# A two-layer transformer block kernel: gate projections of the convolution moved among the heads, its norm into the output projections, and an opening in column groups

## What is computed

```
mod = silu(c) @ w_ada[l] + b_ada[l]                 # shift, scale, gate; the same for the context
h   = rms_norm(x, norm_g[l]) * (1 + scale) + shift
(a_glu, a_gate, nq, nk, nv, n_gate, wq, wk, wv, w_gate, merge) = split(h @ w_in[l])
# convolution branch
a   = a_glu[:, :512] * sigmoid(a_glu[:, 512:])
a   = silu(layer_norm(depthwise_conv(a, 31 taps), cln_g, cln_b))
y_a = (a * silu(a_gate)) @ w_proj_a
# neighbourhood attention (the leading branch, 8 heads of 64) and window attention
y_b = (o_na * silu(n_gate)) @ w_proj_b
y_c = (o_wa * silu(w_gate)) @ w_proj_c
y   = sigmoid(g_a) * y_a + sigmoid(g_b) * y_b + sigmoid(g_c) * y_c
x   = x + gate * (y @ w_o)
```

## Time and profile before

| | |
|---|---|
| median of three runs | 3160.3 us (3156.06 to 3160.52) |
| the profiled execution | 3154.38 us |
| its span, first to last instruction | 3152.6 us |
| mean granted TensorE clock | 0.995 |
| TensorE busy | 3042.8 us |
| VectorE busy | 1829.4 us |
| ScalarE busy | 1295.9 us |
| GpSimd busy | 263.3 us |

### The profile page before, as it was taken

One profiled execution on the slowest core, in us unless ns is written; L12 is line 12 of the kernel. 1 busy time (PEld: TensorE's weight loads), 2 busy tenths in 40 slices (PEclk: granted clock), 3 DMA queues, 4 the chain that ended last, 5 costly groups with the idle time before them and its releaser, 6 DMA issues.

```text
span 3152.6 us, 37117 instructions
## 1 busy us (share of the span) xinstructions
PE 3042.8 (97%) x14862; PEld 2399.3 (76%) x14862; DVE 1829.4 (58%) x2911; ACT 1295.9 (41%) x2007; POOL 263.3 (8%) x206
## 2 busy tenths in 40 slices
PE   8999999999999998999999999999999999999998
PEld 5877877877788677667777777788887876788887
DVE  5877675255435767684444786666436662566632
ACT  3244523135532344534454474322225667422222
POOL 0011100001100001102110021000003210000000
PEclk9999999999999999999999999999999999999999
DMA  5222132320012322222112233333332310233232
GB/s 207 73 67 74 48 104 92 109 86 28 21 34 77 108 80 77 67 81 69 50 51 78 80 96 94 94 94 94 95 96 86 114 38 1 76 97 95 94 94 74
DMA packets 78732, 251.52 MB, mean 80 GB/s; under 512 B 9120, under 2 KB 11168, under 8 KB 78560
## 3 DMA queue, kind: packets, MB, share of 16 engines
q1 hardware_dynamic: 72672, 227.91, 23.1%
q0 software_dynamic: 5024, 18.09, 1.9%
q10 hardware_dynamic: 864, 3.15, 0.3%
HBM read 247.01 MB, written 2.10 MB: 79 GB/s over the span
## 4 chain that ended last, share of the span: by engine, by line
PE 46%; ACT 4%; DVE 2%; issue 1%; DMA 0%; POOL 0%; DVEq 0%; ACTq 0%
PE PS L1158 32%; PE PS L1796 4%; PE PS L2816 3%; PE PS L2917 1%; PE PS L1920 1%; PE PS L2894 1%; ACT WH L1107 1%; PE PS L2895 1%; PE PS L2876 1%; PE PS L2877 0%; PE PS L2838 0%; ACT L1982 0%; PE PS L2544 0%; ACT L1984 0%; DVE WL L1117 0%
## 5 line engine op out<-in xcount | busy, mean ns | idle before, releaser
L1117 DVE TENSOR_TENSOR WL<-RAW,WH 128x1024 fp32r<-128x1024 f32 (+3 forms) x374 | 424.0, 1135 | 528.4 <-ACT WH L1107 527.6
L1107 ACT ACTIVATE WH<-RAW 128x1024 fp32r<-128x1024 f32 (+3 forms) x397 | 384.6, 972 | 436.0 <-PE PS L1158 332.1
L1796 PE MATMUL PS<-Hh,WH 128*128 128x512 f32 x1376 | 524.4, 381 | 14.5 <-DVE WL L1117 8.0
L1796 PE MATMUL PS<-Hl,WH 128*128 128x512 f32 x1376 | 486.6, 354 | 0.0
L1796 PE MATMUL PS<-Hh,WL 128*128 128x512 f32 x1376 | 485.7, 353 | 0.0
L1796 PEld LDWEIGHTS PS<-Hh,WH 128*128 128x128 f32 x1376 | 259.5, 189 | 74.2 <-issue 22.7
L1158 PE MATMUL PS<-XH,WH 128*128 128x512 f32 x768 | 305.0, 397 | 0.0
L1158 PE MATMUL PS<-XH,WL 128*128 128x512 f32 x768 | 303.4, 395 | 0.0
L1158 PE MATMUL PS<-XL,WH 128*128 128x512 f32 x768 | 303.4, 395 | 0.0
L1796 PEld LDWEIGHTS PS<-Hl,WH 128*128 128x128 f32 x1376 | 259.9, 189 | 47.7 <-issue 10.1
L1796 PEld LDWEIGHTS PS<-Hh,WL 128*128 128x128 f32 x1376 | 260.1, 189 | 40.3
(11 more groups left out here) (404 smaller groups left out, 5747.4 us busy)
## 6 DMA issues: line engine op xcount, KB each, us to landing
RAW<-in_w_in SPq DMA_DIRECT2D x124, 512.0 KB, 3.6
RAW<-in_ffn_in SPq DMA_DIRECT2D x96, 512.0 KB, 3.6
RAW<-in_ffn_out SPq DMA_DIRECT2D x48, 512.0 KB, 3.6
RAW<-in_w_ada SPq DMA_DIRECT2D x32, 384.0 KB, 3.7
RAW<-in_nsa_in SPq DMA_DIRECT2D x21, 512.0 KB, 3.3
RAW<-in_lru_in SPq DMA_DIRECT2D x20, 512.0 KB, 3.6
MW<-in_w_ada SPq DMA_DIRECT2D x32, 256.0 KB, 9.6
BS<-in_bs POOLq DMA_DIRECT2D x16, 512.0 KB, 3.9
```

Of the source, the lines that this page charges most:

```text
L1107: act.activation(WH[half[j]][:, 0:n], RAW[j % NRAW][:, 0:n], ACT.Copy).then_inc(*did("act_whi", ("whi", j)))
L1117: dve.tensor_tensor(WL[half[j]][:, 0:n], RAW[j % NRAW][:, 0:n], WH[half[j]][:, 0:n].bitcast(F32), ALU.subtract).then_inc(*did("dve_wlo", ( ...
L1796: mm = pe.matmul(ps[:, c:c + w_], wt[:, 128 * k:128 * k + 128], x[:, a:a + w_], start=(k == 0 and q == 0), stop=(k == n - 1 and q == 2))
```

## The change

In the planner, for layer 1's leading branch: a chunk `cg` of the convolution's gates follows `ag` in phases 1 to 4 (its eviction `cgev` is a Silu after its eighth step, with a reload of the exponential table behind it). The pins of the heads move from step 22 to 27 and that of `out` from 18 to 22. Behind the phases the order is mg3, pj0, pj1, mg4, pj2, mg5, pj3, mg6, pj4, mg7, pj5 to pj7, cm0, pa0, cm1, pa1, and `normed` puts `ln0` behind the last unit of taps, `ln1` four steps later, `lnv`, `ln2`, `ln3` after 10, 14 and 20 steps, and `ln4` one, three and five steps behind pj7. Four fillers go (15 matmuls, 30 instructions): before pv(1,0,0,1,3), max(1,0,2,0,3), pv(1,0,3,0,3) and mg7. The gates' buffer SG of layer 1 moves, and `cgev` in layer 1 no longer waits for the splits.

In the opening: a piece is four matmuls of 128 columns into four column groups, the row copy is four activations, the roots are copied to SBUF by ScalarE (`act_root0`), the first two weight loads go ahead of pieces 16 and 20, their splits come earlier, and `pe_first` computes cb(0,0) and ca(0,0) together, k by k, with pieces 24 to 27 behind k = 2, 28 to 31 behind k = 3 and turn 3 behind k = 4. ScalarE's row copy 2 stands before its first k and row copy 3 before k = 5.

```diff
 KEEP = {
...
-    ('pv', 1, 0, 0, 1, 3): 4,
-    ('max', 1, 0, 2, 0, 3): 2,
-    ('pv', 1, 0, 3, 0, 3): 4,
...
-    ('mg', 1, 0, 7): 5,
...
+        def gates(ph):
+            return [("cg", ph - 1, 1024)] if L else []
...
+            if kind == "cg":
+                return {8: [("cgev", nm)]}
...
-            ready = (25 if L else 19) if br else 22
+            ready = (25 if L else 19) if br else 27 if L else 22
...
-                chunks = [("aq", ph, cq), ("ag", ph - 1, cg), ("av", ph, cv), ("ak", ph + 1, ck) if ph < 3 else ("mg", 0, cm)]
+                chunks = [("aq", ph, cq), ("ag", ph - 1, cg)] + gates(ph) + [("av", ph, cv), ("ak", ph + 1, ck) if ph < 3 else ("mg", 0, cm)]
...
-                chunks = [("ag", 3, cg), ("mg", 1, cm), ("mg", 2, cm)]
+                chunks = [("ag", 3, cg)] + gates(ph) + [("mg", 1, cm), ("mg", 2, cm)]
...
-                    at.setdefault(1 if f else 22 if L and br else 18, []).extend(to)
+                    at.setdefault(1 if f else 22 if L else 18, []).extend(to)
...
+        def normed(units):
+            steps = {0: [("ln0", L)], 4: [("ln1", L)], 10: [("lnv", L)], 14: [("ln2", L)], 20: [("ln3", L)]}
+            begin = max(i for i, u in enumerate(units) if u[0] == "taps")
+            end = sum(u[0] == "lin" for u in units[begin:])
+            steps.update({end + 1: [("ln4", L, 0), ("ln4", L, 1)], end + 3: [("ln4", L, 2)], end + 5: [("ln4", L, 3)]})
+            for m in range(2):
+                units = units + conv_mixed(m)[0:8] + [("mgev", ("cm", L, 0, m))] + conv_mixed(m)[8:] + [("paev", ("pa", L, 0, m))]
...
-            tail += beside(proj(m)) + (beside(merge(m + 4)) if m < 4 else [])
+            ahead_ = m + 3 if L and 1 <= m < 5 else m + 4 if m < 4 and not L else None
+            tail += beside(proj(m)) + (beside(merge(ahead_)) if ahead_ else [])
+        if L:
+            return order + normed(tapped(tail, 1.8) + taps)
...
-                if i == 27:
-                    sp_loads(sp, 1)
+                if i in (15, 19):
+                    sp_loads(sp, i // 16)
...
+        def pe_first(pe):
+            for k in range(8):
+                for kind in ("cb", "ca"):
...
+                    for a, n, c in R768:
+                        for q, (wt, x) in enumerate(((hi, xh), (hi, xl), (lo, xh))):
+                            mm = pe.matmul(ps[:, c:c + n], wt[:, 128 * k:128 * k + 128], x[:, a:a + n], start=(k == 0 and q == 0), stop=(k == 7 and q == 2))
...
+                for i in {2: range(24, 28), 3: range(28, 32)}.get(k, ()):
+                    pe_piece(pe, i)
+                if k == 4:
+                    pe_turn0(pe, 3)
...
-            pe.matmul(rows0(c)[0:2, :], CS[:, 2 * k:2 * k + 2], MW[i % NMOD][:, :], start=(k == 0), stop=(k == 7)).then_inc(*did("pe_mod", ("mm0", i)))
+            for g in range(4):
+                mm = pe.matmul(rows0(c)[32 * g:32 * g + 2, 0:128], CS[:, 2 * k:2 * k + 2], MW[i % NMOD][:, 128 * g:128 * g + 128], start=(k == 0), stop=(k == 7))
+            mm.then_inc(*did("pe_mod", ("mm0", i)))
...
+        def act_root0(act):
+            ps, ri = pairs.of("roots0"), buf("ri0")
+            for q, (a0, n, c) in enumerate(R768):
+                for w in due("act", ("roots",), was("ri0")):
+                    act.wait_ge(*w)
+                act.activation(ri[:, a0:a0 + n], ps[:, c:c + n], ACT.Copy).then_inc(*did("act_rs", ("ri0", q)))
...
             act_row0(act, 1)
-            act_rms(act, "in", HH[0], lambda k, q: MODS[0][:, k, q:q + 1], (2, 1))
+            act_split(act, 0)
+            act_root0(act)
+            act_row0(act, 2)
+            act_rms(act, "in", HH[0], lambda k, q: MODS[0][:, k, q:q + 1], {0: 1, 4: 2})
...
             dve_turn0(dve, 1)
-            dve_rms(dve, "in", HH[0], HL[0], [("roots",)] + [("x", i) for i in range(6)], lambda k, q: AB[:, k, q:q + 1], lambda k, q: MODS[0][:, k, q:q + 1], (2, 1))
+            dve_split(dve, 0)
+            dve_rms(dve, "in", HH[0], HL[0], [("x", i) for i in range(6)], lambda k, q: AB[:, k, q:q + 1], lambda k, q: MODS[0][:, k, q:q + 1], {1: 1, 5: 2})
```

More of the change, by code:

```diff
@@ L341, in begin @@
         self.pairs.take("roots0")
+        self.tmp.take("ri0")
+        self.pairs.release("roots0", ("ri0", 0), ("ri0", 1))
         self.rms("in")
-        self.pairs.release("roots0", ("hx", "in", 7, 1))
+        self.tmp.release("ri0", ("hx", "in", 7, 0), ("hx", "in", 7, 1))
         self.pairs.release("mod0", ("row0", 2), ("row0", 3))
@@ L534, in tick @@
             return ([("modend", L, i // 8 - 2)] if i % 8 == 1 and i > 8 else []) + [("tick", i // 8 - 1, i % 8)]
+        def normed(units):
+            steps = {0: [("ln0", L)], 4: [("ln1", L)], 10: [("lnv", L)], 14: [("ln2", L)], 20: [("ln3", L)]}
+            begin = max(i for i, u in enumerate(units) if u[0] == "taps")
+            end = sum(u[0] == "lin" for u in units[begin:])
+            assert end > 20
+            steps.update({end + 1: [("ln4", L, 0), ("ln4", L, 1)], end + 3: [("ln4", L, 2)], end + 5: [("ln4", L, 3)]})
+            for m in range(2):
+                units = units + conv_mixed(m)[0:8] + [("mgev", ("cm", L, 0, m))] + conv_mixed(m)[8:] + [("paev", ("pa", L, 0, m))]
+            out, n = [], 0
+            for i, u in enumerate(units):
+                out.append(u)
+                if i >= begin:
+                    n += i > begin and u[0] == "lin"
+                    out += steps.pop(n, [])
+            assert not steps
+            return out
         def merge(m):
@@ L559, in branch @@
         order += [("ln4", L, 3)]
-        for m in range(3 if L else 9):
-            if m < (2 if L else 8):
+        for m in range(9):
+            if m < 8:
                 order += beside(lin("cm", m, 4864) + [("mgev", ("cm", L, br, m))])
@@ L1250, in dve_rms @@
                 for q, (a0, n, c) in enumerate(ranges):
-                    for w in due("dve", ("ab0", k // 2) if begin else ("r1", 0, "done"), was(("h", sq, k)), need):
+                    for w in due("dve", [("ab0", k // 2), ("ri0", q)] if begin else ("r1", 0, "done"), was(("h", sq, k)), need):
                         dve.wait_ge(*w)
@@ L1255, in dve_rms @@
                     low(k - 1)
-                if split and k == split[0]:
-                    dve_split(dve, split[1])
+                if split and k in split:
+                    dve_split(dve, split[k])
             low(7)
@@ L1271, in act_rms @@
                         act.activation(hh[:, k, a0:a0 + n], h[:, a0:a0 + n], ACT.Identity, bias=bias_of(k, q)).then_inc(*did("act_h", ("hh", sq, k, q)))
-                if split and k == split[0]:
-                    act_split(act, split[1])
+                if split and k in split:
+                    act_split(act, split[k])
         def border_root(q):
@@ L1372, in pe_begin @@
                     pe_piece(pe, 2 * i - 1)
-            for i in range(8, 32):
+            ps = pairs.of("roots0")
+            for i in range(8, 24):
                 pe_piece(pe, i)
-                if i in (9, 17, 25):
+                if i in (9, 18):
                     pe_turn0(pe, i // 8 - 1)
-                if i == 18:
-                    ps = pairs.of("roots0")
+                if i == 17:
                     for w in due("pe", ("dg",), ("co",), pairs.after["roots0"]):
@@ L1383, in pe_begin @@
                     mm.then_inc(*did("pe_sq", ("roots",)))
+            pe_turn0(pe, 2)
+        def pe_first(pe):
+            for k in range(8):
+                for kind in ("cb", "ca"):
+                    name = (kind, 0, 0)
+                    ps, j = pairs.of(name), P.wj[name, 0]
+                    hi, lo = WH[half[j]], WL[half[j]]
+                    xh, xl = hsrc(0)(k)
+                    for w in due("pe", ("wlo", j), pairs.after[name], hneed(0)(k)):
+                        pe.wait_ge(*w)
+                    for a, n, c in R768:
+                        for q, (wt, x) in enumerate(((hi, xh), (hi, xl), (lo, xh))):
+                            mm = pe.matmul(ps[:, c:c + n], wt[:, 128 * k:128 * k + 128], x[:, a:a + n], start=(k == 0 and q == 0), stop=(k == 7 and q == 2))
+                    if k == 7:
+                        mm.then_inc(*did("pe_lin", ("wfree", j), ("lin", name)))
+                for i in {2: range(24, 28), 3: range(28, 32)}.get(k, ()):
+                    pe_piece(pe, i)
+                if k == 4:
+                    pe_turn0(pe, 3)
         def pe_turn(pe, i):
@@ L1599, in pe_conv @@
             here("pe", ("conv", L))
-            FIRST = {(0, 0): {2: lambda: pe_turn0(pe, 3)}, (1, 0): {2: lambda: pe_tick(pe, 3, 5), 4: lambda: pe_tick(pe, 3, 6), 6: lambda: pe_tick(pe, 3, 7)}}
-            for m in range(4):
+            FIRST = {(1, 0): {2: lambda: pe_tick(pe, 3, 5), 4: lambda: pe_tick(pe, 3, 6), 6: lambda: pe_tick(pe, 3, 7)}}
+            if L == 0:
+                pe_first(pe)
+            for m in range(1 - L, 4):
                 pe_linear(pe, ("cb", L, m), hsrc(L), RX[L], hneed(L), FIRST.get((L, m)))
```

19 lines of the change are left out of this document (11 added, 8 removed).

## The result

| | before | after |
|---|---|---|
| median of 16 runs each, on one chip | 3157.53 us (3154.90 to 3160.52) | 3162.59 us (3158.68 to 3170.79) |
| ratio to before, 95% interval | 1 | 1.0020 [1.0013, 1.0026] |
| the profiled execution | 3154.38 us | 3162.61 us |
| its span | 3152.6 us | 3160.8 us |
| mean granted TensorE clock | 0.995 | 0.988 |

The change makes the kernel slower by 0.2%, 6.3 us by the ratio (4.1 to 8.2). The forecast was 3159.2 us against a median of 3160.3, so -1.1 us; the chances were 0.35 faster, 0.41 the same, 0.24 slower.

What follows compares the result with a forecast made beforehand. TensorE, busy 97% of the span, was taken as the bound, but VectorE behind layer 1's heads. Terms -6.5 - 4.5 + 2.7 + 5.2 + 2.0 = -1.1 us, from median 3160.3 to 3159.2; range 3149 to 3169.

Steps and rivals of the forecast that it cites:

- Opening: -6.5 forecast: Opening: cheaper pieces and earlier products end the first pair at 59.2 us instead of 65.7; bounds -9.5 and -3.
- are there at 1.7 + 10.95/0.385 = 30.1 us: Opening: x, ctx, constants, two weight loads and pieces 0 to 23 have arrived by 30.1 us, so first Hh at 31.2.
- the root copy to SBUF and the first split fall before 30 and hide behind the DMA: Opening: copying the roots and the first weight split finish before 30 us, hidden behind the transfers.
- 1 us of low clock: Opening: TensorE idles 3 us twice, so 1 us is added for reduced clock, giving an end at 59.2.
- rival (c): Opening: column groups do not overlap, eight pieces cost 6.9 us instead of 2.4; sum +3.4, 3164 us; chance 0.04.
- Heads: -4.5 forecast: Layer 1 heads: removed fillers and shorter waits for STAT, Pb, Pa and QB save 4.5 us; bounds 0 and -12.9.
- +2.7 for the tables: Layer 1 heads: four Silu evictions with table loads delay scores by 0.7 us each, +2.7 us; bounds 0 and 12.7.
- Rival (a): Layer 1 heads close up: all 12.9 us go and table loads fall in ScalarE's waits; 3151 us; chance 0.32.
- Rival (b): Layer 1 heads: each gate eviction on ScalarE is fully exposed, 12.7 us instead of 2.7; 3169 us; chance 0.20.
- Stage: +5.2: Stage behind layer 1's heads: with VectorE's queue as bound, net 5.2 us slower; bounds +3.5 and +7.
- +2.0 of clock: Stage behind the heads: half clock after the 10 us wait at the mean's matmul costs 2.0 us; bounds 0 and 4.5.
- norm, Silu and the products with the gates lie beside those steps: Stage, after the mean: this work fits beside 41.4 us of TensorE steps, as VectorE needs 30 us.

Runs made afterwards that it cites:

- open_pieces2: open_only with pieces 24 to 27 behind k = 0, 28 to 31 behind k = 1, turn 3 behind k = 2, row copy 3 before k = 4; 0.9972 of before.
- open_only: The change's opening alone, with layer 1's planner, fillers and gate evictions as in the kernel before; 0.9986 of before, -4.4 us.
- layer1_only: The change's layer 1 part alone, with the opening of the kernel before; 1.0035 of before, +11.1 us.
- combined_maxima: open_pieces2's opening with 14 fillers, layer 1 of taps_in_heads, and layer 1's first two maxima ahead of nrm3 again; 3135.69 us, 0.9932 of before.
- gates_copied: Kernel after, with layer 1's four convolution gate evictions as plain copies, without Silu and its table loads; 1.0013 of before.
- norm_later: Kernel after, with layer 1's mean matmul, variance, root and scaling 14 steps later; 1.0004 of before.
- taps_in_heads: norm_later with cm0, cm1 before pa0, pa1, the old merge order, and taps behind every 4 steps of the heads instead of 5; 0.9980 of before.
- mean_kept_warm: Kernel after, with 17 filler matmuls ahead of the mean's matmul (ln1) in layer 1; 1.0018 of before.

## Why the prediction was wrong

The direction was wrong, since four steps cost more than they were given. Between the two profiles the terms miss the forecast by +4.2 us in the opening, +3.3 between the opening and the heads, -0.7 in the heads, +3.2 in the stage behind them and -0.6 in the rest: 9.4 us, which leads from -1.1 to the +8.2 of the profiles (to rounding; +6.3 by the ratio).

**Opening: -6.5 forecast, -2.3 at the mark in the profile after, -4.4 measured alone.** The step that failed first is the arrival of x, ctx, the constants, two weight loads and pieces 0 to 23, which "are there at 1.7 + 10.95/0.385 = 30.1 us". The transfers had moved that many bytes by about 30.2 us (the GB/s of the first 30 us add up to 10.87 MB), but the transfers of pieces 24 to 31 had been issued too, by 28.5 us, and so the bytes were probably not all of the pieces up to 23. Piece 23 came at 32.1 (`open_pieces2`), row copy 2 began at 32.9 instead of 30.1, the first Hh at 34.0 instead of 31.2, and the first product at 36.3 instead of 33.3. The step beside it, "the root copy to SBUF and the first split fall before 30 and hide behind the DMA", failed too: turn 1 stands behind the roots, which took 2.93 us at half clock, the root copy fell at 30.4 and the split at 31.9. But by `open_pieces2`, where neither was late, that is at most 0.7 of the 3.0 us. From there on the steps kept their distance up to turn 3, 52.1 (forecast 49.0). The end at 63.4 (59.2) holds another 1.1 us: 0.6 from turn 3 to the next product, and 1.6 us of half clock in the last three k where 1.0 was forecast. "SBUF reads cheaper", the reason of the lower bound, did not come: an operation that reads the roots from SBUF takes 0.74 us, one that read them from PSUM 0.75. VectorE's stop for turn 3 had been foreseen, and that it could be ordered away was missed: `open_pieces2` gains twice as much with the same work. The "1 us of low clock" had four stretches against it; TensorE waited for data in part of the first three, and what those cost the end is not shown. Column groups overlap as forecast and rival (c) is out: pieces 28 to 31 stand between 48.77 and the next product within 1.0 us, where (c) had 3.4.

**Between the opening and the heads: nothing forecast, +3.3 in the profile after.** The prediction carried the opening's gain to the heads without a term. Two stretches at half clock that before did not have, 1.7 us each, took 3.4. They are no sure consequence of the change (last section); in `open_only`, where the gain at the mark was 3.6 us, the heads began 1.2 us earlier than before.

**Heads: -4.5 forecast, with +2.7 for the tables, -1.8; measured -2.5 in the profile after and +0.5 in `layer1_only`, -1.5 over five profiles of each kind.** The net is nearly right, its parts are not, so that is luck. The waits did not shrink by a third: the four kinds named grew from 8.3 to 11.5 us, all idle time from 16.8 to 18.6, and without the table loads it is 2.7 us less. The fillers' 4.7 us (20 instructions at 1.89 for 8) went in full, and one to three stretches of half clock of 1.7 us each came, where the heads of before have none or one. Rival (a), the heads close up, is out: the room per unit grew, but the waits hang on what stands ahead on VectorE's and ScalarE's queues, as `combined_maxima` shows with one step of one list. Its price was also summed wrongly: with the table loads in ScalarE's own waits the 2.7 us go too, which makes 3148, below the stated range. Rival (b) is out too by `gates_copied`: it needed 12.7 us exposed, 3.6 came back.

**Stage: +5.2 and +2.0 of clock forecast, +10.4 measured.** The queue of VectorE was read rightly: T + 37.4 forecast for the mean's matmul, T + 37.2 measured; 10 us forecast for that wait, 9.5 measured; 3.7 before mg4, 3.3 measured. (That all waits together come to 15.3 forecast and 15.7 measured is partly luck: the 1.6 us for pj3 did not come, and 2.0 for the products with the gates did. The prediction's own terms also add up to T + 81.9, not 82.1.) With the clock the end was forecast at T + 84.1 and came at T + 88.0, all of it behind the mean. Two steps failed there. The term of the clock, "+2.0 us", was laid at one wait only; 3.9 us came, 2.3 behind the mean and 1.6 behind the waits for the products with the gates. And "norm, Silu and the products with the gates lie beside those steps" put at nothing what cost two waits of 1.02 us: ScalarE and VectorE take turns in these products, and TensorE reached them first. Clock 1.9 us over its term and waits 2.0 us over nothing make the 3.9 us; against before 0.7 less of it counts, as before ended at T + 100.2 by the mark and not at T + 99.5.

**What is shown and what is not.** That layer 1 carries the loss is shown by `layer1_only` and `open_only`; that VectorE's queue made the waits of its stage, by `norm_later` and `taps_in_heads`; that the opening's start hangs on piece 23 and its stop on the order, by `open_pieces2`. The share of half clock is read from single profiles, and the one trial on it, `mean_kept_warm`, moved too little to prove it. The time measured lies inside the range of 3149 to 3169; the direction was wrong, and "slower" at 0.24 was too low for a change that takes out fillers and adds waits of 3 and 10 us.

## What to carry to other kernels

Moving work between engines' queues changes who stands ahead of whom; read, for each moved unit, the two or three instructions in front of it on every queue before crediting it with cover. Price every new wait of some microseconds twice, once for itself and once for the clock behind it, the second only where the engine does not wait again right behind. Ask of a transfer when its own bytes land, not when the sum of bytes has passed. And put work of the engine that is the bound (here VectorE's taps) where that engine has gaps before reordering the engine that waits. A stop on one engine can often be ordered away at no cost: moving eight pieces, a turn and a row copy by one or two k gave 4.4 us here, as much as the whole new opening had (uncertain by as much).
